# Stick-breaking attention: scores for one head at a time, and the sum over later blocks as two fp32r products

## The reference, cut to what matters

```python
z = jnp.einsum('bhtd,bhsd->bhts', q_blk, k_blk) * scale
strict = s_pos < t_pos
log_beta = jax.nn.log_sigmoid(z)
log_1m_beta = jnp.where(strict, jax.nn.log_sigmoid(-z), 0.0)
between = lax.cumsum(log_1m_beta, axis=3, reverse=True) - log_1m_beta
weights = jnp.where(strict, jnp.exp(log_beta + between), 0.0)
outs.append(jnp.einsum('bhts,bhsv->bhtv', weights, v_blk))
```

## Time and profile before

| | us |
|---|---|
| median of 3 runs | 2455.09 (2452.5 to 2456.87) |
| the profiled execution | 2456.69 |
| its span | 2454.9 |
| what lies around the span | 1.8 |
| the stage: first scores (2203.14) to the last product of the first w_out tile (2358.69) | 155.55 |

### The profile page before, as it was taken

One profiled execution on the slowest core, in us unless ns is written; L12 is line 12 of the kernel. 1 busy time (PEld: TensorE's weight loads), 2 busy tenths in 40 slices (PEclk: granted clock), 3 DMA queues, 4 the chain that ended last, 5 costly groups with the idle time before them and its releaser, 6 DMA issues.

```text
span 2454.9 us, 45626 instructions
## 1 busy us (share of the span) xinstructions
PE 2363.5 (96%) x17622; PEld 1881.5 (77%) x17622; DVE 1389.8 (57%) x1747; ACT 939.0 (38%) x1418; POOL 1294.0 (53%) x768
## 2 busy tenths in 40 slices
PE   7999979999999999999999999999999999998798
PEld 5777769996877788888888877887877777773367
DVE  4377685556257666666665434564454366655464
ACT  3133352222335444444444212232252135557641
POOL 3332100001666677777777789789676445530045
PEclk9999999999999999999999999999999999999999
DMA  4311000000432333333332655465321111122033
GB/s 146 80 37 34 27 16 4 5 4 19 146 113 94 120 111 111 108 115 116 110 107 92 234 199 189 168 209 186 130 92 62 45 48 48 53 73 86 1 118 122
DMA packets 106616, 231.79 MB, mean 94 GB/s; under 512 B 7368, under 2 KB 46664, under 8 KB 106312
## 3 DMA queue, kind: packets, MB, share of 16 engines
q1 hardware_dynamic: 82496, 169.89, 20.8%
q10 hardware_dynamic: 23944, 59.46, 7.5%
HBM read 190.52 MB, written 38.80 MB: 93 GB/s over the span
## 4 chain that ended last, share of the span: by engine, by line
PE 73%; DVE 9%; ACT 6%; POOL 5%; issue 3%; DMA 3%; ACTq 0%; DVEq 0%; POOLq 0%; SPq 0%
PE ps L834 11%; PE ps L1310 6%; PE ps L1311 6%; PE ps L1312 6%; PE ps L1467 6%; PE ps L930 5%; PE ps L1439 4%; PE ps L1490 3%; PE ps L1348 2%; PE ps L1350 2%; PE ps L1351 2%; DMA w_raw<-wall 2%; POOL w_lo L621 2%; ACT ab L152 2%; POOL w_hi L618 2%
## 5 line engine op out<-in xcount | busy, mean ns | idle before, releaser
L618 POOL TENSOR_TENSOR w_hi<-w_raw,small 128x1024 fp32r<-128x1024 f32 x156 | 305.9, 1961 | 738.4 <-PE ps L834 274.6
L621 POOL TENSOR_TENSOR w_lo<-w_raw,w_hi 128x1024 fp32r<-128x1024 f32 x156 | 431.2, 2764 | 12.3
L683 POOL TENSOR_TENSOR slot_lo<-scr,slot_hi 128x512 fp32r<-128x512 f32 x116 | 160.6, 1395 | 85.5 <-ACT slot_hi L152 85.5
L834 PE MATMUL ps<-x_hi,w_hi 128*128 128x512 f32 x448 | 176.0, 402 | 5.3 <-POOL w_lo L621 2.3
L834 PE MATMUL ps<-x_lo,w_hi 128*128 128x512 f32 x448 | 172.1, 393 | 0.0
L834 PE MATMUL ps<-x_hi,w_lo 128*128 128x512 f32 x448 | 172.0, 393 | 0.0
L152 ACT ACTIVATE slot_hi<-scr 128x512 fp32r<-128x512 f32 x116 | 73.4, 633 | 195.6 <-POOL scr L693 77.7
L1310 PE MATMUL ps<-t_hi,slot_hi 128*128 128x512 f32 x348 | 135.5, 389 | 0.4 <-ACT p L152 0.4
L1311 PE MATMUL ps<-t_lo,slot_hi 128*128 128x512 f32 x348 | 135.4, 389 | 0.0
L1312 PE MATMUL ps<-t_hi,slot_lo 128*128 128x512 f32 x348 | 135.4, 389 | 0.0
L639 POOL COPY xx<-rmask 128x512 f32<-128x512 f32 x16 | 11.8, 749 | 227.5 <-PE ps L1133 174.6
(11 more groups left out here) (389 smaller groups left out, 6471.9 us busy)
## 6 DMA issues: line engine op xcount, KB each, us to landing
w_raw<-wall SPq DMA_DIRECT2D x191, 512.0 KB, 3.5
f_raw<-f_spill SPq DMA_DIRECT2D x62, 512.0 KB, 4.5
f_spill<-cg SPq DMA_DIRECT2D x30, 512.0 KB, 3.4
v_raw<-wall SPq DMA_DIRECT2D x29, 512.0 KB, 3.5
ada_w<-wada ACTq DMA_DIRECT2D x24, 512.0 KB, 3.9
fill_spill<-stage ACTq DMA_DIRECT2D x24, 256.0 KB, 2.0
x_in<-xT ACTq DMA_DIRECT2D x8, 512.0 KB, 8.8
x<-xT ACTq DMA_DIRECT2D x8, 512.0 KB, 4.2
```

What stands on the lines that cost most here:

```text
L618: nc.gpsimd.tensor_tensor(w_hi[:, u, :, :], w_raw[:, u, :, :], sm["one"].unsqueeze(2).to_broadcast([P, KT, P]), ALU.mult).then_inc(S("w_hi ...
L621: nc.gpsimd.tensor_tensor(w_lo[:, u, :, :], w_raw[:, u, :, :], w_hi[:, u, :, :].bitcast(F32), ALU.subtract).then_inc(S("w_split"), 1)
L683: tt_p(slot_lo[i][:, :, :], src, slot_hi[i][:, :, :].bitcast(F32), ALU.subtract).then_inc(later("s_lo")[0], 1)
L834: last = mm(ps[:, 2 * u + h, :], w[:, u, k, :], x[:, k, h * 512:(h + 1) * 512], start=(k == 0 and w is w_hi and x is hi), stop=(k == KT - ...
```

## The change

Four things are done.

Scores by head. `scores_of(n)` makes the scores of one head and `mask_of(n)` its mask; `sb_z` counts heads. From b = 3 on, the two halves of a head's queries lie on different partition halves, so that the halves of one head, not the two heads, go through PE side by side. For that the queries are loaded with the halves of one partition group exchanged, by four DMAs of 64 partitions beside one for the keys, and a turned copy of the first 512 keys of each head (`k_turn`) is loaded by four DMAs from ACT's queue behind `soft(1)`. In PE's order each head whose bank is free by the head rule (`z_ahead_head`) stands before `remainder(2m)`, the others after `weigh(m-1)`.

On PE, around the scores of the first step with two banks and the next (blocks 3 and 2 of pass one): before, `spl` of head 8 (128 and 512 columns) is next after head 7.

```diff
-            def z_scores(m):
-                p, b = SB_STEPS[m]
-                if z_free(m):
-                    pe.wait_ge(S("sb_w"), z_free(m))
+            def scores_of(n):
+                p, b = SB_STEPS[n // 2]
+                e = n % 2
+                if z_free_head(n):
+                    pe.wait_ge(S("sb_w"), z_free_head(n))
...
                 for x, c, t in halves_of(b):
-                    for e, q in enumerate((slice(0, 64), slice(64, P))):
-                        mm(z_out(2 * m + e, x)[:, c:], proj2[q, 11 + p, b * P:(b + 1) * P], proj2[q, 9 + p, t],
-                           start=True, stop=True, skip_group_check=True)
-                for e in range(2):
-                    last = mm(z_out(2 * m + e, b // 4)[:, b % 4 * P:(b % 4 + 1) * P], eye16[:, :], past16[:, :], start=False,
-                              stop=True, skip_group_check=True)
-                last.then_inc(S("sb_z"), 1)
+                    g = e if x else 1 - e
+                    q = slice(64 * g, 64 * g + 64)
+                    keys = proj2[q, 11 + p, b * P:(b + 1) * P] if x else k_turn[p][q, b * P:(b + 1) * P]
+                    mm(z_out(n, x)[:, c:], keys, proj2[q, 9 + p, 512 * e + c:512 * e + 512],
+                       start=True, stop=True, skip_group_check=True)
+            def mask_of(n):
+                b = SB_STEPS[n // 2][1]
+                mm(z_out(n, b // 4)[:, b % 4 * P:(b % 4 + 1) * P], eye16[:, :], past16[:, :], start=False,
+                   stop=True, skip_group_check=True).then_inc(S("sb_z"), 1)
...
                 if b < NB - 1:
-                    pe.wait_ge(S("sb_acc"), n - 1)
+                    pe.wait_ge(S("sb_acc"), sums_made(n - 2))
                     for x, c, t in halves_of(b + 1):
-                        last = mm(z_out(n, x)[:, c:], sbmask[:, 1, :], lacc[:, e, t], start=False, stop=True,
+                        mm(z_out(n, x)[:, c:], ones_r[:, :], acc_hi[:, e, t], start=False, stop=True, skip_group_check=True)
+                        last = mm(z_out(n, x)[:, c:], ones_r[:, :], acc_lo[e][:, t.start - P:t.stop - P], start=False, stop=True,
                                   skip_group_check=True)
...
             for m in range(len(SB_STEPS)):
-                if z_ahead(m + 1):
-                    z_scores(m + 1)
+                heads = [n for n in (2 * m + 2, 2 * m + 3) if n < 2 * len(SB_STEPS)]
+                z_scores([n for n in heads if z_ahead_head(n)])
                 remainder(2 * m)
                 if m:
                     weigh(m - 1)
-                if m + 1 < len(SB_STEPS) and not z_ahead(m + 1):
-                    z_scores(m + 1)
+                z_scores([n for n in heads if not z_ahead_head(n)])
                 remainder(2 * m + 1)
...
+            def sums_split(n):
+                b, e = SB_STEPS[n // 2][1], n % 2
+                if b == 0:
+                    return
+                vcopy(acc_hi[:, e, b * P:], lacc[:, e, b * P:])
+                tt(acc_lo[e][:, (b - 1) * P:], lacc[:, e, b * P:], acc_hi[:, e, b * P:].bitcast(F32), ALU.subtract)\
+                    .then_inc(S("sb_acc"), 1)
```

More of the change, by code:

```diff
@@ L94 @@
     "in_a": ("bias_in", "rmask_in") + tuple(f"x_again{k}" for k in range(8)) + ("gmask_in", "sbmask_in"),
-    "in_b": ("smask_in", "smask2_in", "qk_back") + tuple(f"x2_back{k}" for k in range(8)),
+    "in_b": ("smask_in", "smask2_in") + tuple(f"qk_back{k}" for k in range(5)) + tuple(f"x2_back{k}" for k in range(8)),
 }
@@ L347, in build @@
         past16 = at("past16", [P, P], 49, BF16, off=spare + 256)
+        k_turn = [at("k_turn0", [P, 512], 48), stage]
         past_in = at("past_in", [P, P], 49, off=spare + 512)
@@ L352, in build @@
         lacc = at("lacc", [P, 2, T], 10)
-        sq_h = [at("sq_h", [P, 4, T], 6)[:, k, :] for k in range(4)] + [at("sq_h2", [P, 2, T], 16)[:, k, :] for k in range(2)]
+        sq_h = [at("sq_h", [P, 4, T], 6)[:, k, :] for k in range(4)] + [at("sq_h2", [P, 2, T], 14)[:, k, :] for k in range(2)]
+        acc_hi = at("acc_hi", [P, 2, T], 16, F32R)
+        acc_lo = [at("acc_lo0", [P, T - P], 45, F32R), at("acc_lo1", [P, T - P], 49, F32R, off=spare + 512)]
+        ones_r = at("ones_r", [P, P], 45, F32R, off=3584)
         gate_a = at("gate_a", [P, 6, T], 35)
@@ L416, in z_free, with z_free_head, z_ahead_head @@
                        default=0)
+        def z_free_head(n):
+            return max([k + 1 for k in range(n) if set(z_banks(k)) & set(z_banks(n))], default=0)
+        def z_ahead_head(n):
+            return n < 2 * len(SB_STEPS) and z_free_head(n) <= 2 * (n // 2 - 1)
         def z_ahead(m):
@@ L1567, in z_scores @@
                     pe.wait_ge(S("hn_log"), 3 * (p + 1))
+                    pe.wait_ge(S("past_in"), 80)
                 for x, c, t in halves_of(b):
[L1569 to L1575 removed]
+                    g = e if x else 1 - e
[7 more added lines that the diff above has]
+                   stop=True, skip_group_check=True).then_inc(S("sb_z"), 1)
+            def z_scores(heads):
+                for n in heads:
+                    scores_of(n)
+                for n in heads:
+                    mask_of(n)
             def weigh(m):
@@ L2351, in _ @@
                         act.wait_ge(S("d_done"), 15 * NB)
-                        act.dma_start(proj2[:, 9:13, :], fill_dram[0:4].rearrange("k p t -> p k t")).then_inc(landed("qk_back")[0], 16)
+                        act.dma_start(proj2[:, 11:13, :], fill_dram[2:4].rearrange("k p t -> p k t"))\
+                            .then_inc(landed("qk_back0")[0], 16)
+                        for g in range(2):
+                            for e in range(2):
+                                act.dma_start(proj2[64 * g:64 * g + 64, 9:11, hc(e)],
+                                              fill_dram[0:2][:, 64 * e:64 * e + 64, hc(int(g == e))].rearrange("k p t -> p k t"))\
+                                    .then_inc(landed(f"qk_back{1 + 2 * g + e}")[0], 16)
                     if b and l == 2:
@@ L2405, in _ @@
             soft(1)
+            act.wait_ge(S("stage_out"), 16 * 2 * N_FILL)
+            for p in range(2):
+                for e in range(2):
+                    q = slice(64 * (1 - e), 64 * (1 - e) + 64)
+                    act.dma_start(k_turn[p][q, :], fill_dram[2 + p][64 * e:64 * e + 64, 0:512]).then_inc(S("past_in"), 16)
             output(NB - 1)
@@ L3205, in _ @@
                         soft(n + 2)
+                    sums_split(n)
                     if n == 8:
```

18 lines of the change are left out of this document (11 added, 7 removed).

## The result

The changed kernel takes 2459.51 us in the median of 22 runs, the kernel before 2453.97 in 22 runs beside them: a ratio of 1.0023, with a 95% interval of 1.0015 to 1.0031. That is 5.6 us slower, where 3.5 were forecast. The profiled execution took 2461.93 us, its span is 2460.2.

What follows compares the result with a forecast made beforehand. It took a ring through PE, ACT and DVE as the bound, with DVE's chain setting the wide stretches after the change. 3.5 - 2.0 + 3.6 - 0.5 - 1.1 = +3.5 us gave 2458.6 on the median, range 2451 to 2466.

Steps and rivals of the forecast that it cites:

- DVE's price: On DVE, added casts of 0.49, 0.56, 0.63 us and subtractions of 0.825, 0.958, 1.092 us at the three widths.
- The dear cast: Rival: DVE's cast runs at the two-source rate, 1.1 us at 896 columns; +5.3 us, 2463.9; chance 0.17.
- DVE as the bound: In both wide stretches DVE's work plus gaps sets the length, 38.2 and 33.5 us; chance 0.55.
- The second stretch: Sum of head 8 to softplus of head 17: DVE's chain 38.2 us of 40.15, a gain of 2.0.
- The fourth: Sum of head 24 to softplus of head 31: DVE's chain 33.5 us against 33.99, a gain of 0.5.
- The block at heads 10 and 26: Waiting scores stand before the remainder in PE's queue: head 8's sum 3.5 us late, 2.1 lost at heads 24 to 26.
- Three small terms: Losses in stretches one and three: head 0's split 0.4 us, halves of heads 8, 9 0.6, of heads 24, 25 0.6.
- Stretch three: Softplus of head 17 to sum of head 24, 33.78 us: a loss of 3.6, scores of head 18 1.3 later.
- stretch one: Up to the sum of head 8, 34.79 us: a loss of 3.5; turned keys' issues, 1.5, hidden in a wait.
- The fifth stretch: After the softplus of head 31, 12.84 us: remainder 31 is 0.7 shorter, in all a gain of 1.1.
- The clock: Rival: two more PE clock falls behind waits before heads 10 and 26 cost 3.4 us: 2462.0; chance 0.15.
- ACT as the bound: Rival: ACT sets the wide stretches, 32.4 and 29.3 us; sum -6.4 us, 2448.7; chance 0.13.

Runs made afterwards that it cites:

- e8: e3 with each DVE subtraction of the wide heads made twice, same result; ratio to the kernel before 1.0067.
- e6: e3 with three DVE squares moved out of the first wide stretch to heads 5 and 16; ratio to the kernel before 1.0006.
- e3: Changed kernel with the scores of heads 10 and 26 behind the remainder of heads 8 and 24 in PE's queue; ratio to the kernel before 1.0014.
- e5: Changed kernel with the four loads of turned keys issued by SyncE instead of ACT; ratio to the kernel before 1.0031.
- e2: Kernel before with only the split sums: two fp32r all-ones products, DVE casts and subtractions; ratio to the kernel before 1.0029.
- e1: Changed kernel with one plain fp32 all-ones product instead of the split, no cast or subtraction; ratio to the kernel before 1.0014.
- e11: e9 with one plain fp32 all-ones product, without cast and subtraction; ratio to the kernel before 0.9993.
- e9: Changed kernel with the edits of e3, e5 and e6, and the first stage's outputs moved out of the wide stretches; ratio to the kernel before 0.9998.
- e10: Kernel before with only the moved squares and first-stage outputs of e9; ratio to the kernel before 1.0006.
- e12: e1 with the edits of e3, e5 and e6, first-stage outputs at their old places; ratio to the kernel before 0.9955.

## Why the prediction was right or wrong

The time fell on the forecast's side and near its number: 5.6 us slower where 3.5 stood. Its terms did less well. By stretch it had +3.5, -2.0, +3.6, -0.5 and -1.1, and the profiles show +6.5, -0.2, +1.8, -1.2 and +0.1: the stage is 7.0 us longer, twice the forecast, and errors of up to 3.0 us partly cancel. So the nearness of the number is in part luck, and a term that it had left to a rival came in.

**DVE's price was right.** Cast 627 ns and subtraction 1092 at 896 columns, against 0.63 and 1.09; 33.76 and 29.52 us of work. The dear cast is out. By the rule of the Trainium skill that the prediction drew on, "VectorE: DVE Perf Modes", section on what auto-detection checks, this cast can go at two elements a cycle; the measured pair agrees: from 128 to 896 columns the cast grows by 400 ns, from 227 to 627, and the subtraction by 800, from 292 to 1092.

**DVE as the bound was right**, as e8's dose and e6's relief show for e3's order. ACT no longer waits for scores before heads 10, 12 and 14, as was said, but for the remainder before `wts` 10 to 13: 2.25, 0.68, 0 and 0.23 us. The second stretch came to 39.92 instead of 38.2: the excess is the 1.68 us that DVE waits at its end for the remainder of head 15, which stands in PE's queue behind that of head 14, whose triangle took 3.78 us instead of 1.98. The fourth came to 32.80 against 33.5, as DVE's gaps were 3.3 us and not 4.0.

**The block at heads 10 and 26 was right in place and wrong in size.** From the end of the softplus of head 9 to the sum of head 8 it is 3.79 us against 0.16, so 3.63 where 2.5 was the share of the sum: the remainder behind it runs at half clock. At head 26 the same difference is 1.58 (2317.90 - 2316.16 against 0.16) where 2.1 stood; PE waited 1.25 us there, not nearly 3.

**Three small terms failed.** The split of head 0 ahead of the square (0.4) and the halves of heads 8 and 9 and of 24 and 25 (0.6 and 0.6) cost nothing: e5 has the split, the halves of heads 8 and 9 and the old first stretch. PE's rows show why for the halves: the scores of heads 8 and 9 run from 2230.4 to 2231.7, and the 128 columns of a head run beside its 512. That is 1.35 us, what the two heads side by side took in the earlier trace rows, and the scores of heads 24 and 25 take the same.

**Stretch three came to 35.60 instead of 37.4.** Its first term was right in kind and too small: the scores of head 18 come 1.9 us later against the cut, not 1.3 (0.72 behind it, 1.14 ahead of it before). What the sum did not have is the fourth head mean, at half clock in the kernel before (3.17 us) and not here (1.94).

**The failed step of stretch one is "The four turned keys cost ACT 4 x 0.38 = 1.5, in a wait of 1.54".** Each issue took 0.6 us, 2.4 in all, so 1.74 us showed; and PE, which then waited 3.90 us, made the head mean at half clock, 1.57 us more. Together that is 3.3, a little more than the 2.9 us of the table's first column.

**The fifth stretch was wrong:** 12.91 instead of 11.7. The triangle of head 30 at half clock, 3.61 us, holds up PE, and that of head 31 begins 1.46 us behind the last softplus instead of 0.66: the 0.7 us that the shorter product wins is spent there. The row of before:

```profile
2346.51 1.98 PE L1594 MATMUL ps<-spl,sbmask 128*128 128x512 f32 x4
```

**The clock is the term that was missing from the sum.** The prediction put it aside as a rival with two more falls behind the new waits. One of its readings against it was wrong, "Other waits in the stage as long are not followed by one": no other wait of PE there is as long as 2.38 us; of the two next, one of 2.00 ahead of the first head mean is not followed by a fall, and one of 2.01 is. In the kernel before:

```profile
2302.55 1.35 PE L1570 MATMUL ps<-proj 64*128 64x128 f32 x8 [2.01 <-ACT sq_h L152]
...
2304.03 2.02 PE L1594 MATMUL ps<-spl,sbmask 128*128 128x512 f32 x2
```

That triangle, of head 22, is at half clock in both kernels (2.02 and 1.98 us). In the changed kernel there are five other places: the first head mean, the remainder of head 8, and the triangles of heads 10, 14 and 30, each behind a wait of PE of 1.04 to 4.04 us. An estimate from the rows is the length of each stretch times what its PEclk lacks of 1.00: 11.9 us in all here, 3.4 in the earlier trace rows. That is 8.5 us more, against 7.0 by which the stage is longer.

Over all runs, three pairs differ in the split of the sum and what goes with it: the mean clock is 0.9846 before and 0.9804 in e2, 0.9829 in e1 and 0.9818 in the changed kernel, 0.9840 in e11 and 0.9818 in e9. The nine kernels with the split have mean clocks from 0.9788 to 0.9828, the four others of the table from 0.9829 (e1) to 0.9860, the kernel before 0.9845. In the 96 runs of the kernel before, 0.001 of mean clock goes with 2.1 us (median 2458.4 at 0.982, 2448.7 at 0.987); 0.001 of the whole time is 2.5 us. At the changed kernel's 0.9818 that line gives 2459.0, near the 2459.5 that it takes; at 0.983 the median is 2455.4 for it (4 runs) and 2456.8 for the kernel before (18). Read so, the slower clock goes with the whole difference, and the other gains and losses cancel. The same reading fits e9, whose medians at 0.982, 0.983 and 0.984 (3, 3 and 1 runs) lie 4.6 to 5.9 us under the kernel before's, while its time as a whole is the same. This is a correlation over runs: no run here changed the clock alone, and a longer wait costs time by itself besides. Why the clock is lower with the split was not tried. In the first wide stretch PEclk is 1.00 in the kernel before, e10, e11 and e12, 0.96 in e1, which has no split but the block at head 10, and 0.84 to 0.96 in the nine with the split.

**The rivals.** ACT as the bound didn't come, for the reason given. e12, without the split and with three repairs, shows what it might have been: 35.85 and 31.81 us, so even then some 3 us over ACT's 32.4 and 29.3.

## What to carry to other kernels

An edit that takes a wait away lengthens the chain that was next; work out that chain's busy time plus its gaps in the stage itself, and if it comes to the stretch's length the edit gains little until that engine is relieved. Cheaper products on an engine that others wait for went with a lower clock here, so compare the granted clock of both kernels, over many runs, before the times. Where two edits come as one change, run each alone and then repair the one that survives: here the scores by head came to 11 us under the kernel before, some 5 of them at the same clock, once the split was gone, the new loads were issued by an idle queue, one instruction list was put in another order and three squares were moved.

## What the runs showed of the hardware that was not expected

A DVE cast from one SBUF tensor is held up by a GpSimd addition that began before it: 1.82 us instead of 0.49 beside an addition of 1.54. GpSimd's copy behind the addition stands beside the cast in turn, ends 0.15 us behind it and takes 0.56 us, where with no cast beside it such a copy takes 0.29. The Trainium skill, "SBUF — State Buffer", section on who interferes with whom, says that such a fast one-source operation and one of GpSimd exclude each other for the whole instruction, by order of issue, and the trace agrees: the cast ends 0.36 us behind the addition.

PE's first head mean waits for the same square in all fourteen executions. In the six that issue the turned keys from ACT the wait is 3.7 to 4.0 us and the mean takes 2.94 to 3.68 us, never 1.94. In the eight others the wait is 2.0 us, and the mean takes 1.94 in six and 2.44 and 3.10 in two. The fourth mean waits 2.3 to 2.4 us in all fourteen; it takes 1.94 in five of them and 2.57 to 3.63 in nine, the kernel before among these. So the same wait is followed by a fall in one execution and by none in the next, and a single profile prices a stretch to no better than 1.7 us for each such place.
